# One stage in place of two at the head of a two-layer step: x turned unscaled beside the first modulation, scale and shift applied to turned feature tiles

## The reference, cut to what matters

```
mod = silu(c) @ w_mod[0] + b_mod[0]          # one vector of 6*1024 for latent, one for context tokens
shift1, scale1, gate1, shift2, scale2, gate2 = split(mod, 6)
h = rms_norm(x, g_pre1) * (1 + scale1) + shift1
proj = h @ w_in[0]                           # 1024 -> 1968 columns, then mixers, output projection, channel mixer
```

## Time and profile before

| | us |
|---|---|
| median of 3 runs | 2095.58 |
| profiled execution, its own time | 2096.19 |
| its span in the trace | 2094.4 |
| PE busy | 1939.1 (93%) |
| DVE busy | 1296.8 (62%) |
| ACT busy | 1045.0 (50%) |
| first matmul of the input projection starts | 54.32 |

### The profile page before, as it was taken

How to read it: one execution, slowest core, us unless ns; L and a number is a source line. 1 busy time by engine, 2 the same in 40 slices (tenths; PEclk the granted TensorE clock), 3 DMA queues, 4 the chain that set the end, 5 groups by cost and what they waited for, 6 DMA issues and landing times. The chain is left out here.

```text
span 2094.4 us, 32083 instructions
## 1 busy us (share of the span) xinstructions
PE 1939.1 (93%) x11352; PEld 1622.5 (77%) x11352; DVE 1296.8 (62%) x1958; ACT 1045.0 (50%) x1689; POOL 95.9 (5%) x62
## 2 busy tenths in 40 slices
PE   4998899899999999997998999887999999999993
PEld 2996555599999998986986555876888888888883
DVE  3725656574323323356627565656888888888886
ACT  4214444454112111144235254546888888888884
POOL 0330000000000000001300000002000000000001
PEclk9999999899999999998999999898999999999997
DMA  6205502202223213213125601158967191826464
GB/s 253 95 26 200 201 34 93 106 11 81 66 81 96 81 61 91 72 40 104 57 81 214 267 1 41 62 196 335 410 253 302 69 354 50 337 105 265 175 245 160
DMA packets 130339, 302.25 MB, mean 144 GB/s; under 512 B 17984, under 2 KB 63936, under 8 KB 127296
## 3 DMA queue, kind: packets, MB, share of 16 engines
q1 hardware_dynamic: 124240, 279.10, 36.5%
q10 hardware_dynamic: 3120, 11.28, 1.4%
q0 software_dynamic: 2880, 10.49, 1.3%
HBM read 358.73 MB, written 28.61 MB: 185 GB/s over the span
## 5 line engine op out<-in xcount | busy, mean ns | idle before, releaser
L2267 DVE TENSOR_TENSOR ex_wl<-ex_raw,ex_wh 128x1024 fp32r<-128x1024 f32 x351 | 419.8, 1220 | 32.7 <-ACT ex_wh L2145 22.2
L2145 ACT ACTIVATE ex_wh<-ex_raw 128x1024 fp32r<-128x1024 f32 x351 | 368.1, 1060 | 79.5 <-PE psum L2202 48.1
L2546 PE MATMUL psum<-norm_out,ex_w_hi 128*128 128x320 f32 x1408 | 269.0, 309 | 3.8 <-PEq L1586 3.8
L2202 PE MATMUL psum<-ex_wh,ex_he_hi 128*128 128x512 f32 (+1 forms) x624 | 243.6, 390 | 11.1 <-DVE ex_wl L2267 11.1
L2202 PE MATMUL psum<-ex_wl,ex_he_hi 128*128 128x512 f32 (+1 forms) x624 | 233.7, 375 | 0.0
L2202 PE MATMUL psum<-ex_wh,ex_he_lo 128*128 128x512 f32 (+1 forms) x624 | 233.3, 374 | 0.0
L2546 PEld LDWEIGHTS psum<-norm_out,ex_w_hi 128*128 128x128 f32 x1408 | 223.3, 188 | 4.1 <-DVE ex_w_lo L2417 4.0
L2417 DVE TENSOR_TENSOR ex_w_lo<-side,ex_w_hi 128x1024 fp32r<-128x1024 f32 (+1 forms) x82 | 82.6, 1014 | 165.0 <-ACT ex_w_hi L2413 164.8
L2546 PE MATMUL psum<-norm_out,ex_w_lo 128*128 128x320 f32 x704 | 165.8, 308 | 0.0
L2202 PEld LDWEIGHTS psum<-ex_wh,ex_he_hi 128*128 128x128 f32 x624 | 118.3, 190 | 33.5 <-issue 9.2
L2202 PEld LDWEIGHTS psum<-ex_wh,ex_he_lo 128*128 128x128 f32 x624 | 118.6, 190 | 22.1 <-issue 2.9
(11 more groups left out here) (406 smaller groups left out, 3825.5 us busy)
## 6 DMA issues: line engine op xcount, KB each, us to landing
ex_raw<-moe_gate_up SPq DMA_DIRECT2D x221, 512.0 KB
ex_raw<-moe_w_down SPq DMA_DIRECT2D x143, 512.0 KB
x<-moe_gate_up SPq DMA_DIRECT2D x65, 512.0 KB
wmod_ssd<-w_mod SPq DMA_DIRECT2D x56, 512.0 KB, 6.3
wmod_at<-w_mod SPq DMA_DIRECT2D x24, 512.0 KB, 4.3
side<-ffn_w_gate SPq DMA_DIRECT2D x22, 512.0 KB, 3.8
side<-ffn_w_up SPq DMA_DIRECT2D x22, 512.0 KB, 3.8
mx_qkv_room<-w_in SPq DMA_DIRECT2D x10, 1024.0 KB, 5.0
```

Of the source, the lines that this page charges most:

```text
L2145: act.activation(wh[:, i % RING], raw_of(i), ACT.Copy).then_inc(*hi_done.up(1))
L2202: last = pe.matmul(p.psum[:, 2 + g % 2, 0:width], h[:, k], w[:, i % RING, cols], start=(k == 0 and m == 0), stop=(k == KD - 1 and m == 2))
L2267: dve.tensor_tensor(wl[:, i % RING], raw_of(i), wh[:, i % RING].bitcast(F32), ALU.subtract).then_inc(*lo_done.up(1))
L2546: last = pe.matmul(p.psum[:, home[i] + half, 0:HT], m[:, i % w.RING, cols], x[:, k, half * HT:(half + 1) * HT], start=(k == 0 and n == 0), ...
```

## The change

The two first stages become one, `stage_first_norm`. The list of what is different:

- Statistics: 5 pairs of square and root on ScalarE and 5 inversions on VectorE, one per block, in place of 5 squares, one root and one inversion.
- Turning: x is scaled by 1/rms on ScalarE (1024 columns at a time), turned by 8 transposes per block, and copied out of PSUM without scale or shift, 512 columns in one instruction, one half by VectorE (L386 of the new program), one by ScalarE (L323).
- On TensorE the order is unit 0, blocks 0 to 2, unit 1, blocks 3 and 4, unit 2, unit 3. Units are now ordered so that units 0 and 1 give shift and scale of features 0 to 511, units 2 and 3 those of the rest.
- Scale and shift are applied per feature tile over all 640 tokens (512 latent, 128 context), twice: ScalarE writes the rounded high part (L328), VectorE writes the whole value (L400) and from it the low part (L404). This is done in two halves of 4 tiles (`affine`), the first between units 1 and 2 on VectorE, the second after unit 3.
- The modulation's ring lies where the high and low parts of w_in will be, so ScalarE splits piece 0 only after all units. Piece 0 is loaded behind the modulation's quarters on SP, piece 1 only in the next stage.
- One barrier goes.

```diff
-def stage_first_modulation(p):
+def stage_first_norm(p, h, turned, side, weights, at):
...
+        mod = Modulation(p, [(0, u) for pair in zip(first, scale) for u in pair], 0, own, "first", 8, banks=4, at=at)
...
                 mod.load(sp)
+                weights.load(sp, 0)
...
+                def take_far(b):
+                    act.wait_ge(*norm.turned.at(b + 1))
+                    act.activation(block_of(b, 0), in_psum(b, 0), ACT.Copy).then_inc(*norm.far.up())
+                def keep_high(k):
+                    for lo, hi, s in spans:
+                        last = act.activation(norm.hi[:, k, lo:hi], turned[:, k, lo:hi], ACT.Identity,
+                                              scale=p.scale_in[:, 0, 0, k, s:s + 1], bias=p.mod[:, 0, k, s:s + 1])
+                    last.then_inc(*norm.high.up())
...
+                for b in range(TB):
+                    norm.statistics(act, b, x_in.at(32))
+                norm.scale(act, 0)
+                for b in range(TB):
+                    if b + 1 < TB:
+                        norm.scale(act, b + 1)
+                    take_far(b)
...
+                for half in range(2):
+                    act.wait_ge(*scales.at(half + 1))
...
+                    for k in range(HALF * half, HALF * (half + 1)):
+                        keep_high(k)
+                act.wait_ge(*mod.used.at(MM_STEPS * len(mod.units)))
+                weights.split_hi(act, 0)
...
+                unit(0)
+                for b in range(3):
+                    turn(b)
+                unit(1)
+                for b in range(3, TB):
+                    turn(b)
+                unit(2)
+                unit(3)
...
+                def affine(half):
+                    part = slice(HALF * half, HALF * (half + 1))
+                    dve.wait_ge(*mod.taken.at(2 * half + 2))
...
+                    for k in range(HALF * half, HALF * (half + 1)):
+                        if k >= 2:
+                            dve.wait_ge(*norm.low.at(k - 1))
+                        for lo, hi, s in spans:
+                            last = dve.tensor_scalar(whole[:, k % 2, lo:hi], turned[:, k, lo:hi], p.scale_in[:, 0, 0, k, s:s + 1],
+                                                     p.mod[:, 0, k, s:s + 1], ALU.mult, ALU.add)
+                        link(dve, last)
+                        dve.wait_ge(*norm.high.at(k + 1))
+                        dve.tensor_tensor(norm.lo[:, k], whole[:, k % 2], norm.hi[:, k].bitcast(F32),
+                                          ALU.subtract).then_inc(*norm.low.up())
...
+                for b in range(3):
+                    norm.invert(dve, b)
+                unit(0)
+                for b in range(3, TB):
+                    norm.invert(dve, b)
+                for b in range(2):
+                    take_near(b)
+                unit(1)
+                for b in range(2, TB):
+                    take_near(b)
...
+                affine(0)
+                unit(2)
+                unit(3)
+                affine(1)
+                weights.split_lo(dve, 0)
...
-                for i in pieces[2:]:
+                for i in pieces[1 if l == 0 else 2:]:
                     w.load(sp, i)
```

More of the change, by code:

```diff
@@ L168, with __init__ @@
 class Modulation:
-    def __init__(self, p, units, bank, own, tag, ring, banks=1):
+    def __init__(self, p, units, bank, own, tag, ring, banks=1, at=None):
         self.p, self.units, self.bank, self.banks, self.ring = p, units, bank, banks, ring
         if units:
-            self.w = p.sb(f"wmod_{tag}", [P, ring, QK * UNIT], ctx=own)
+            shape = [P, ring, QK * UNIT]
+            self.w = p.sb(f"wmod_{tag}", shape, ctx=own) if at is None else p.placed(f"wmod_{tag}", shape, F32, at)
             self.row = p.sb(f"modrow_{tag}", [P, UNIT], ctx=own)
@@ L262, in modulation_units, with bank, block_of, in_psum @@
     return units[0:2 + TB], units[2 + TB:]
-def stage_first_modulation(p):
+def stage_first_norm(p, h, turned, side, weights, at):
     nc, io = p.nc, p.io
     x_in, vectors_in, dve_c = p.sig("x_in"), p.sig("vectors_in"), p.sig("dve_chain")
-    consts, pool_chain, silu_done, wide_ready = (p.sig(n) for n in (
-        "consts", "pool_chain", "silu_done", "silu_wide_ready"))
-    squared, mean, root = p.sig("x_squared"), p.sig("x_mean"), p.sig("x_root")
+    consts, pool_chain, silu_done, wide_ready, scales = (p.sig(n) for n in (
+        "consts", "pool_chain", "silu_done", "silu_wide_ready", "first_scales"))
+    HALF = KD // 2
     with ExitStack() as own:
-        mod = Modulation(p, [(0, u) for u in range(2 * D // UNIT)], 0, own, "first", 8, banks=4)
+        first, scale = range(0, D // UNIT), range(D // UNIT, 2 * D // UNIT)
+        mod = Modulation(p, [(0, u) for pair in zip(first, scale) for u in pair], 0, own, "first", 8, banks=4, at=at)
         p.silu_wide = p.sb("silu_wide_first", [P, KD, 32], ctx=own)
-        junk, far = p.sb("fm_junk", [P, D], ctx=own), p.sb("far", [P, 2, P], ctx=own)
+        far = p.sb("far", [P, 2, P], ctx=own)
+        norm = Norm(p, 0, 0, h, True, side[:, 0:D], scaled=side[:, D:2 * D])
+        whole = side[:, 2 * D:2 * D + 2 * T].rearrange("p (r t) -> p r t", r=2)
+        spans = ((0, LAT, 0), (LAT, T, 1))
+        def bank(b):
+            return 4 + 2 * (b % 2)
+        def block_of(b, half):
+            return turned[:, HALF * half:HALF * (half + 1), b * P:(b + 1) * P]
+        def in_psum(b, half):
+            return p.psum[:, bank(b) + half].rearrange("p (k t) -> p k t", k=HALF)
         with nc.Block() as block:
@@ L305, in _, with unit, turn @@
                 act.activation(p.silu_c, p.silu_c, ACT.Silu).then_inc(*silu_done.up())
+                act.wait_ge(*consts.at(1))
                 for b in range(TB):
-                    squares_of(p, act, b, junk[:], x_in.at(32), squared)
-                root_of_means(p, act, mean, root)
+                    norm.statistics(act, b, x_in.at(32))
[4 more added lines that the diff above has]
+                    take_far(b)
+                act.wait_ge(*norm.far.at(TB))
+                for half in range(2):
+                    act.wait_ge(*scales.at(half + 1))
+                    if half:
+                        act.wait_ge(*norm.near.at(TB))
+                    for k in range(HALF * half, HALF * (half + 1)):
+                        keep_high(k)
+                act.wait_ge(*mod.used.at(MM_STEPS * len(mod.units)))
+                weights.split_hi(act, 0)
             @block.tensor
             def _(pe):
+                def unit(n):
+                    for step in range(UNIT_STEPS * n, UNIT_STEPS * (n + 1)):
+                        mod.on_tensor(pe, step)
+                def turn(b):
+                    if b >= 2:
+                        pe.wait_ge(*norm.near.at(b - 1))
+                        pe.wait_ge(*norm.far.at(b - 1))
+                    norm.turn(pe, b, bank(b))
                 pe.wait_ge(*wide_ready.at(1))
                 pe.wait_ge(*consts.at(1))
-                for step in range(len(mod.steps)):
-                    mod.on_tensor(pe, step)
+                unit(0)
[6 more added lines that the diff above has]
+                unit(3)
             @block.vector
@@ L319, in _, with unit, take_near @@
                 link = chained(dve_c)
+                def unit(n):
+                    for step in range(UNIT_STEPS * n, UNIT_STEPS * (n + 1)):
+                        mod.on_vector(dve, step)
+                def take_near(b):
+                    dve.wait_ge(*norm.turned.at(b + 1))
+                    dve.tensor_copy(block_of(b, 1), in_psum(b, 1)).then_inc(*norm.near.up())
+                def affine(half):
+                    part = slice(HALF * half, HALF * (half + 1))
+                    dve.wait_ge(*mod.taken.at(2 * half + 2))
+                    dve.scalar_tensor_tensor(
+                        out=p.scale_in[:, 0, 0, part], in0=p.mod[:, 0, KD + HALF * half:KD + HALF * (half + 1), :], scalar=1.0,
+                        in1=p.gains[:, 0, 0, part].to_broadcast([P, HALF, 2]), op0=ALU.add, op1=ALU.mult).then_inc(*scales.up())
+                    dve.wait_ge(*scales.at(half + 1))
+                    for k in range(HALF * half, HALF * (half + 1)):
[8 more added lines that the diff above has]
+                                          ALU.subtract).then_inc(*norm.low.up())
                 link(dve, dve.memset(p.silu_wide[:], 0.0))
@@ L325, in _ @@
                 dve.tensor_copy(p.silu_wide[:, :, 0:2], p.silu_c).then_inc(*wide_ready.up())
[L326 to L420, removed]
@@ new lines, in _ @@
+                for b in range(3):
[8 more added lines that the diff above has]
+                    take_near(b)
+                dve.wait_ge(*norm.far.at(TB))
+                dve.wait_ge(*norm.near.at(TB))
+                affine(0)
+                unit(2)
+                unit(3)
@@ L523, in keep_low @@
                           ALU.subtract).then_inc(*self.low.up())
```

(1 more changed line is left out.)

7 lines of the change are left out of this document (3 added, 4 removed).

## The result

| | kernel before | changed kernel |
|---|---|---|
| median | 2097.21 us (5 runs) | 2107.49 us (5 runs, 2105.70 to 2109.60) |
| ratio | | 1.0054, 95% interval 1.0043 to 1.0065 |
| span of the profiled execution | 2094.4 | 2105.7 |
| first matmul of the input projection | 54.32 | 64.38 |
| from there to the span's end | 2040.1 | 2041.3 |

By these medians the change costs 10.3 us. The ratio is estimated from all runs and is not the quotient of the two medians (that would be 1.0049); by it the cost is 11 us, 9 to 14. In the traces 10.1 us are there when the input projection starts; the forecast was 8.8. The median of the kernel before rose from 2095.58 to 2097.21 with two more runs, which is the other part of the distance between 2104.4 forecast and 2107.49 measured.

A forecast was written before the change was run, and what follows sets the result against it. Waiting for x and weights, then pre-norm, bound the start of the input projection; the chain of statistics, turns, units, affine halves and split ends at 63.1, +8.8 us, so median 2095.6 becomes 2104.4, range 2099 to 2110.

The forecast's parts named there:

- Statistics to 22.4: New first stage, ScalarE: five blocks of square and root at 1.38 us from 14.13, plus 1.3, end at 22.4.
- Scale and turn alternate, first two turns slow: Blocks 0 to 2: one tile prevents overlap; two turns take 1.94, the third 1.04; 8.9 us, block 2 turned at 31.3.
- rival 2: TensorE at the low clock all through until 54 us: +13.7 us, 2109.3; chance 0.14.
- Unit 1 at full clock, 2.14: Behind block 2's turn on TensorE: unit 1's 16 matmuls start at 31.3 and take 2 x 1.07 us.
- A feature tile 1.58 us: Affine part on VectorE: each feature tile takes 1.58 us, bounds 1.45 and 1.85; a half of four tiles 6.7.
- Units 2 and 3 at the low clock, 8.1 from row copy to sums: After the first affine half: copies, transposes, unit 3 and sums all run at low clock, 8.1 us, to 53.9.
- Start at 63.1: End of the new first stage: split and barrier done, input projection starts at 63.1, 8.8 us later than before.
- The DMA share falls between 23 and 31: First stage: with x and 12 quarters (8.6 MB) landed, DMA stands nearly idle from about 22 to 31 us.
- The input projection keeps its length: Input projection: old length, 111 us to its last matmul; piece 1 ready 11.3 after the start, cost 0, at worst 1.
- rival 4: Input projection: piece 1 lands in 10 rather than 5 us, +2 us on top, 2106.5; chance 0.05.
- Rival 1: First stage: TensorE at full clock all through, +4.4 us, 2100.0; chance 0.15.
- Rival 3: Turning hidden on TensorE between units 0 and 2, the last weights set the end: -11.7 us, 2083.9; chance 0.06.

The follow-up runs named there:

- e8: Changed kernel with piece 1 of the projection's weights loaded behind piece 0 in the first stage again; median 2108.69 us, ratio to the kernel before 1.0059.
- e4: Changed kernel with 98 data-free identity transposes filling TensorE's gaps; median 2100.84 us, ratio to the kernel before 1.0025.
- e5: Changed kernel with TensorE's order as weights land, two tiles for scaled x, unit 3's VectorE work between first feature tiles; median 2094.21 us, ratio to before 0.9991.
- e7: Kernel before the change with 60 identity transposes on TensorE behind the last turned block, until the barrier; median 2095.81 us, ratio 0.9999.

## Why the prediction was right, point by point

- **Statistics to 22.4.** The root of block 4 ended at 22.31 in the changed kernel. Right.
- **Scale and turn alternate, first two turns slow.** Right in kind; the third too was slow (1.94). Block 2 was turned at 31.97, not 31.3. This part of rival 2 held for one more block.
- **Unit 1 at full clock, 2.14.** Mis-sized: 3.46. At full clock these 16 matmuls take 1.92 (unit 2), and the transposes right behind them took 0.66, as at full clock: the clock rose only during unit 1. With the third turn this is +1.9 at the start of the affine part (41.0 for 39.1).
- **A feature tile 1.58 us.** 1.58. ScalarE's first high part cost 0.56 and 0.49 per half where I had 0.2. By the Trainium skill's page VectorE: DVE Perf Modes, section Mode 2×_2P, a one-source fp32 operation in SBUF gives two results per cycle. The trace agrees for the two-scalar form: 543 ns for 512 columns and 342 for 128, that is 0.52 ns for each further column, and 0.80 us for both together, where the two-source L404 takes 826 ns for 640 columns.
- **Units 2 and 3 at the low clock, 8.1 from row copy to sums.** It was 6.7 (48.04 to 54.78). The transposes of unit 2 took 1.12 as taken, but the clock came back within unit 3 (3.04 for 3.86), and the second transposes took 0.66. -1.4.
- **Start at 63.1.** 64.38. The terms: +0.7 turn, +1.2 unit 1, +0.6 ScalarE's first parts, -1.4 units 2 and 3, and 0.2 in roundings. The chain is the one forecast, but that its end is off by no more than 1.3 us is partly luck: 2.5 us of terms too small stand against 1.4 of one too large.
- **The DMA share falls between 23 and 31.** It was nothing from about 25 to 33 us, with the next quarters issued at 33.9. The bytes had been added up too low: 640 tokens of x are 2.6 MB and 12 quarters 6.3, so 8.9 MB, not 8.6. Nothing hangs on it.
- **The input projection keeps its length.** 111.79 us against 111.69, and e8 found no cost of the moved load. POOL had the low part of piece 1 ready 11.5 us after the start (75.91), where the sum had 11.3, so rival 4, a late piece 1, did not come. The first step of the first convolution took 1.81 us (VectorE, at 74.46) while POOL split piece 1 (71.31 to 75.91), against 0.55 before and 0.56 in e8, where POOL was done by then. That is the overlap that the prediction had named, and nothing waited for it.
- **Rival 1** (full clock) was priced at +4.4. e4 came nearest: start +4.35, median +4.1. That the numbers are the same is luck, since the rival took 4.4 from 8.8 and e4 took 5.7 from 10.1. **Rival 3** (turning hidden) was priced at a start of 42.6; no experiment got there, the nearest is e5 at 49.88, because block 4 isn't turned before 31.9 even with both chains undone, and 12.6 us of feature tiles follow.
- **Rival 2** (low clock all through) was priced at +13.7. It held up to the third turn and for most of unit 1, but the fourth and fifth turn took 1.04 and 1.07 us, so the rest of it did not come.

What the runs tell apart is that two parts of the order cost, not the operations: PE's list holds units behind turns, and the single tile makes turns slow. That a chain of statistics starts only when x lands at 14.1 was argued from the rows and no run removes it. One more cause stayed untested: ScalarE's list has all five statistics ahead of the first scale. In the changed kernel 1/rms of block 0 is there at 17.04 and its scale starts at 22.22; no run put scales between the statistics.

## What to carry to other kernels

Before work is moved ahead of a late transfer, add up the chain that it brings along: it must fit in the time that is left, and whatever it stands in front of in an engine's list can start only when it has ended. Here unit 1, which had begun at 19.27, was put behind a chain that ends at 31.97, and as the ring's slots came free only with it, the last four loads stood still too. Put such work behind each transfer's own consumers, in their gaps, and double the tile through which two engines alternate.

## What the runs showed of the hardware that I had not expected

The rest of the program, which but for the load of piece 1 is the same in all ten kernels, took 2038.7 to 2045.9 us in the ten profiled executions. Part of this is where the low clock falls. In e5 and the kernel before, the end of the stage behind the projection holds the same work: 32 matmuls and 4 transposes. Windows (PE busy, clock, DMA share, GB/s), e5 first; the last window of the kernel before also holds the first matmuls of the next stage:

```profile
229.00:233.00 4.00, 1.37 (x8) 0.72 0.01 2
233.00:237.00 4.00, 4.00 (x21) 0.50 0.00 0
237.00:241.00 4.00, 2.73 (x13) 0.50 0.00 0
```

```profile
234.00:238.00 4.00, 1.36 (x8) 0.80 0.00 0
238.00:242.00 4.00, 4.00 (x29) 0.77 0.00 0
242.00:246.00 4.00, 1.53 (x13) 1.00 0.20 18
```

In e5 the granted clock is 0.72, 0.50 and 0.50 over 12 us, in the kernel before 0.80, 0.77 and 1.00, and TensorE had been idle for 2.9 us ahead of this work in both. The work takes 8.1 us in e5 (from 231.63) and 5.9 in the kernel before (from 236.64); its second 16 matmuls alone take 3.68 and 2.00. Stage by stage such differences are up to 2 us, and they are of the size of what e5 and e7 gained at the projection's start and didn't show in the median. They vary from run to run in one and the same kernel: e5's eleven runs reach from 2091.5 to 2097.6, the four fastest with a mean granted clock of 0.964 to 0.966, the four slowest with 0.962 to 0.964, and the profiled one is the slowest. Whether an earlier start also brings them about is open. A gain of 2 to 4 us in one stage of this kernel can be read in a trace, and not safely in the total.
